# Two feed-forward layers on the unnormed x, with the reciprocal mean square put on the second product, and one plain weight tile in place of two

## The reference

```python
def rms_norm_2(x, w):
    xf = x.astype(jnp.float32)
    y = xf * lax.rsqrt(jnp.mean(xf * xf, axis=-1, keepdims=True) + RMS_EPS)
    return (y * w.astype(jnp.float32)).astype(x.dtype)

    for layer in range(DEPTH_2):
        ...
        x = x + mixed @ w_out[layer]
        h = rms_norm_2(x, mlp_norm_w[layer])
        x = x + jnp.square(jax.nn.relu(h @ w_up[layer])) @ w_down[layer]
    return rms_norm_2(x, final_norm_w)
```

## Time and profile before

| | us |
|---|---|
| median of 3 runs | 1392.38 (1392.15 to 1392.46) |
| the profiled execution, as a whole | 1391.14 |
| its span, from the first to the last instruction | 1389.4 |
| PE busy | 1369.2 (99%) |
| DVE busy | 649.9 (47%) |
| ACT busy | 263.4 (19%) |
| granted TensorE clock, mean | 0.998 |

### The profile page before, as it was taken

One profiled execution on the slowest core, in us unless ns is written; L12 is line 12 of the kernel. 1 busy time (PEld: TensorE's weight loads), 2 busy tenths in 40 slices (PEclk: granted clock), 3 DMA queues, 4 the chain that ended last, 5 costly groups with the idle time before them and its releaser, 6 DMA issues.

```text
span 1389.4 us, 21701 instructions
## 1 busy us (share of the span) xinstructions
PE 1369.2 (99%) x9138; PEld 1051.1 (76%) x9138; DVE 649.9 (47%) x1483; ACT 263.4 (19%) x561; POOL 7.2 (1%) x16
## 2 busy tenths in 40 slices
PE   9999999999999999999999999999999999999997
PEld 6888886454445444454488879999998878999997
DVE  2476554111111111111287837775446784777544
ACT  2234102000000000000143421220004352122000
POOL 0000000000000000000000000000000000000000
PEclk9999999999999999999999999999999999999999
DMA  9895667999999999999944234444544414444510
GB/s 392 352 390 227 255 242 292 421 421 420 421 421 421 420 421 420 421 421 420 421 169 152 90 118 159 179 164 171 171 163 152 152 62 150 154 168 166 177 67 32
DMA packets 51235, 362.53 MB, mean 261 GB/s; under 512 B 6064, under 2 KB 6384, under 8 KB 7872
## 3 DMA queue, kind: packets, MB, share of 16 engines
q1 hardware_dynamic: 48528, 353.39, 64.4%
q10 hardware_dynamic: 2032, 5.70, 1.4%
q0 software_dynamic: 576, 2.01, 0.4%
HBM read 357.92 MB, written 1.06 MB: 258 GB/s over the span
## 4 chain that ended last, share of the span: by engine, by line
PE 95%; DMA 3%; DVE 1%; issue 0%; SPq 0%; ACT 0%; DVEq 0%
PE bank L1096 26%; PE bank L844 23%; PE bank L546 20%; PE bank L558 5%; PE bank L854 4%; PE bank L832 4%; DMA ring<-in_weights 3%; PE bank L1241 2%; PE bank L1032 2%; PE bank L663 2%; PE bank L1145 1%; PE bank L1196 1%; PE bank L1222 1%; PE bank L1209 1%; PE bank L884 0%
## 5 line engine op out<-in xcount | busy, mean ns | idle before, releaser
L546 PE MATMUL bank<-h,ring 128*128 128x256 f32 x832 | 184.5, 381 | 0.1
L546 PEld LDWEIGHTS bank<-h,ring 128*128 128x128 f32 x832 | 156.7, 190 | 22.5 <-issue 1.5
L844 PE MATMUL bank<-ring,x_s 128*64 128x512 f32 x768 | 167.8, 592 | 1.6 <-issue 0.9
L844 PEld LDWEIGHTS bank<-ring,x_s 128*64 128x64 f32 x768 | 56.1, 137 | 110.1 <-issue 110.1
L1096 PE MATMUL bank<-hid,ring 128*128 128x128 f32 x912 | 115.6, 275 | 0.0
L1096 PE MATMUL bank<-h,ring 128*128 128x128 f32 x896 | 113.8, 275 | 0.0
L1096 PEld LDWEIGHTS bank<-hid,ring 128*128 128x128 f32 x912 | 108.6, 192 | 0.0
L1096 PEld LDWEIGHTS bank<-h,ring 128*128 128x128 f32 x896 | 107.0, 192 | 0.1
L1956 DVE TENSOR_TENSOR act<-act,bank 128x512 f32<-128x512 f32 x16 | 11.0, 687 | 195.7 <-PE bank L844 195.7
L1096 PE MATMUL bank<-sq,ring 128*128 128x128 f32 x720 | 95.1, 275 | 0.0
L1096 PEld LDWEIGHTS bank<-sq,ring 128*128 128x128 f32 x720 | 87.6, 192 | 0.0
(11 more groups left out here) (361 smaller groups left out, 1701.3 us busy)
## 6 DMA issues: line engine op xcount, KB each, us to landing
ring<-in_weights SPq DMA_DIRECT2D x288, 1024.0 KB, 12.3
ringx<-in_weights SPq DMA_DIRECT2D x48, 1024.0 KB, 19.8
x<-in_x SPq DMA_DIRECT2D x1, 1024.0 KB, 5.1
pool_a<-in_cst ACTq DMA_DIRECT2D x1, 1024.0 KB, 6.5
bias<-bias_rows POOLq DMA_DIRECT2D x1, 1024.0 KB, 16.6
ring<-cq ACTq DMA_DIRECT2D x8, 128.0 KB, 2.4
ring<-ck ACTq DMA_DIRECT2D x8, 128.0 KB, 2.4
out<-h ACTq DMA_DIRECT2D x2, 512.0 KB, 3.6
```

The costliest lines, as they stand in the source:

```text
L546: ins = e.matmul(u.ap[:, 0:S], w[:, k * width + j * P:k * width + (j + 1) * P], acts[:, k, :], start=k == 0, stop=k == kc - 1)
L844: ins = e.matmul(g.bank[bank][ex * SLOTS:(ex + 1) * SLOTS, :], stat(m)[:, ex * SLOTS:(ex + 1) * SLOTS], pair[ex][:, m * 512:(m + 1) * 512] ...
```

## The change

The feed-forward part of both layers runs on `g.xw` in place of the normed `g.h`. The reciprocal mean square `g.scr2` multiplies the result of the second product ahead of its addition to x. One tile of `w_up` is plain in place of two, and 15 run in seven products in place of 14. The square root and the scaling of `g.h` go. ACT takes over relu and square of the two plain chunks. The squares go to `g.h`. On PE the sum of the squares stands behind seven tile 1 in place of behind the first plain chunk; on the DVE the weight sums of tiles 0 and 1 stand between the additions to x, the differences are made from `g.xw`, and `dve_norm` keeps its place ahead of the loop over the seven tiles.

```diff
-UPS = 14
+PLAIN = 1
+UPS = 16 - PLAIN
 SEVENS = UPS + 15
@@ pe_layer
-    for j in range(2):
-        w = g.filled(e, layer_tile(l, 16 + j))
-        for jj in range(2):
-            oc = 2 * j + jj
-            pe_chunk(e, g, ("up", l, oc), w, jj, 256, KC, g.xw, raw(1))
-            if oc == 0:
-                pe_norm_added(e, g, n + 1)
-        g.owed += 1
+    w = g.filled(e, layer_tile(l, 16))
+    for jj in range(2):
+        pe_chunk(e, g, ("up", l, jj), w, jj, 256, KC, g.xw, raw(1))
+    g.owed += 1
     for i in range(SEVENS):
         pe_seven(e, g, l, i)
+        if i == 1:
+            pe_norm_added(e, g, n + 1)
@@ pe_seven
-    (b11, t1), (b21, b22) = token_quarters(g.h if i < UPS else g.hid[:, 8 * b:8 * b + 8, :])
+    (b11, t1), (b21, b22) = token_quarters(g.xw if i < UPS else g.hid[:, 8 * b:8 * b + 8, :])
@@ act_layer
-        e.activation(g.sq2[:, 2 * j:2 * j + 2, :], g.x[:, 2 * j:2 * j + 2, :], ACT.Square).then_inc(s["squares"], 1)
-    act_root(e, g, 3 + 2 * l, g.rs2, g.scr2)
+        e.activation(g.h[:, 2 * j:2 * j + 2, :], g.x[:, 2 * j:2 * j + 2, :], ACT.Square).then_inc(s["squares"], 1)
+    for jj in range(2):
+        ps = g.full(e, "up", l, jj)[:, 0:S]
+        g.read(("up", l, jj), e.activation(g.hid[:, jj, :], ps, ACT.Relu))
+        g.evac(e, "up", l, jj)
+    e.activation(g.hid[:, 0:2, :], g.hid[:, 0:2, :], ACT.Square).then_inc(s["hid_ready"], 1)
@@ dve_layer
-        if j > 1:
-            dve_add_squares(e, g, n + 1, j - 1, 2)
-    dve_add_squares(e, g, n + 1, 3, 2)
-    dve_weight_sums(e, g, l, 0)
+        if 1 <= j <= 2:
+            dve_weight_sums(e, g, l, j - 1)
+    e.wait_ge(s["xw"], KC * (2 * l + 2))
+    dve_differences(e, g, g.xw, g.h_diff, g.t1_last)
+    for j in range(1, 4):
+        dve_add_squares(e, g, n + 1, j, 2, g.h)
     dve_norm(e, g, n + 1, None, g.h, g.rs2, g.scr2)
-    dve_rs_scaled(e, g, n + 1)
-    e.wait_ge(s["h_scaled"], KC * (n + 2))
-    dve_differences(e, g, g.h, g.h_diff)
-    for oc in range(4):
-        ps = g.full(e, "up", l, oc)
-        g.read(("up", l, oc), e.tensor_tensor(g.hid[:, oc, :], ps[:, 0:S], g.rs2, ALU.mult))
-    for oc in range(4):
-        g.evac(e, "up", l, oc)
-        ins = e.scalar_tensor_tensor(out=g.hid[:, oc, :], in0=g.hid[:, oc, :], scalar=0.0, in1=g.hid[:, oc, :], op0=ALU.max,
-                               op1=ALU.mult)
-    step.up(ins)
-    chunks_done = step.n
-    dve_weight_sums(e, g, l, 1)
     for i in range(SEVENS):
         key, b, of = seven_block(l, i)
...
             two = g.x[:, 2 * mp:2 * mp + 2, :].rearrange("p c t -> p (c t)")
+            e.wait_ge(s["recip"], RECIPS[n + 1])
+            both = g.pair_c.rearrange("p (c t) -> p c t", c=2)
+            g.after(e)
+            step.up(e.tensor_tensor(both, both, g.scr2.unsqueeze(1).to_broadcast([P, 2, S]), ALU.mult))
+            g.after(e)
             ins = e.tensor_tensor(two, two, g.pair_c, ALU.add)
...
-        g.read(("down", l, jj), e.tensor_tensor(g.x[:, k, :], g.x[:, k, :], ps[:, 0:S], ALU.add))
+        g.read(("down", l, jj), e.tensor_tensor(g.pair_a, ps[:, 0:S], g.scr2, ALU.mult))
         g.evac(e, "down", l, jj)
+        e.tensor_tensor(g.x[:, k, :], g.x[:, k, :], g.pair_a, ALU.add).then_inc(s["x_down"], 1)
+        e.wait_ge(s["x_down"], 5 * l + 4 + jj)
```

More of the change, by code:

```diff
@@ L498 @@
 RECIPS = {0: 1, 1: 2, 2: 4, 3: 5, 4: 6, 5: 7, 6: 8}
-ROOTS = {0: 1, 1: 2, 2: 4, 3: 6, 4: 7, 5: 9, 6: 10}
+ROOTS = {0: 1, 1: 2, 2: 4, 4: 6}
 ADDED = {0: 1, 1: 2, 3: 3, 4: 4, 5: 5, 6: 6}
 def pe_norm_added(e, g, n):
-    sq = g.sq2 if n else g.sq
+    sq = {0: g.sq, 3: g.h, 5: g.h}.get(n, g.sq2)
     u = g.take(e, ("ss", n))
@@ L537, in h_ready @@
 def h_ready(e, g, n, k):
-    e.wait_ge(g.s["h_shifted" if n < 2 else "h_scaled"], KC * n + k + 1)
+    e.wait_ge(g.s["h_shifted" if n < 2 else "h_scaled"], KC * (n if n < 2 else 1 + n // 2) + k + 1)
 def pe_chunk(e, g, key, w, j, width, kc, acts, ready, bank=None):
@@ L1037, in pe_layer @@
         g.owed += 1
-    for j in range(2):
-        w = g.filled(e, layer_tile(l, 16 + j))
-        for jj in range(2):
-            oc = 2 * j + jj
-            pe_chunk(e, g, ("up", l, oc), w, jj, 256, KC, g.xw, raw(1))
-            if oc == 0:
-                pe_norm_added(e, g, n + 1)
-        g.owed += 1
+    w = g.filled(e, layer_tile(l, 16))
+    for jj in range(2):
+        pe_chunk(e, g, ("up", l, jj), w, jj, 256, KC, g.xw, raw(1))
+    g.owed += 1
     for i in range(SEVENS):
         pe_seven(e, g, l, i)
-    w = g.filled(e, layer_tile(l, 18 + SEVENS))
-    e.wait_ge(s["hid_ready"], UPS * (l + 1))
+        if i == 1:
+            pe_norm_added(e, g, n + 1)
+    w = g.filled(e, layer_tile(l, 16 + PLAIN + SEVENS))
+    e.wait_ge(s["hid_ready"], 16 * (l + 1))
     for jj in range(2):
@@ L1080, in pe_seven @@
     key, b, of = seven_block(l, i)
-    w = g.filled(e, layer_tile(l, 18 + i))
+    w = g.filled(e, layer_tile(l, 16 + PLAIN + i))
     (a11, a12), (a21, a22) = quarters(w)
     s1, s2, s3, s4 = (g.sums[i % 2][:, n * 512:(n + 1) * 512].rearrange("p (k c) -> p k c", k=4) for n in range(4))
-    (b11, t1), (b21, b22) = token_quarters(g.h if i < UPS else g.hid[:, 8 * b:8 * b + 8, :])
+    (b11, t1), (b21, b22) = token_quarters(g.xw if i < UPS else g.hid[:, 8 * b:8 * b + 8, :])
     t2, t3, t4 = g.h_diff if i < UPS else g.hid_diff[b]
-    if i >= UPS and b == 3:
+    if i < UPS or b == 3:
         t1 = g.t1_last
@@ L1499, in act_layer @@
         g.evac(e, "lout", l, j)
-        e.activation(g.sq2[:, 2 * j:2 * j + 2, :], g.x[:, 2 * j:2 * j + 2, :], ACT.Square).then_inc(s["squares"], 1)
-    act_root(e, g, 3 + 2 * l, g.rs2, g.scr2)
+        e.activation(g.h[:, 2 * j:2 * j + 2, :], g.x[:, 2 * j:2 * j + 2, :], ACT.Square).then_inc(s["squares"], 1)
[4 more added lines that the diff above has]
+    e.activation(g.hid[:, 0:2, :], g.hid[:, 0:2, :], ACT.Square).then_inc(s["hid_ready"], 1)
     for i in range(UPS):
-        two = g.hid[:, 4 + 2 * i:6 + 2 * i, :]
+        two = g.hid[:, 2 + 2 * i:4 + 2 * i, :]
         act_first_product(e, g, ("up7", l, i))
@@ L1520, in act_down @@
         act_first_product(e, g, ("down7", l, k // 2))
[L1521 to L1524, removed]
+    e.wait_ge(g.s["x_down"], 5 * l + (k // 2 if k < 6 else k - 3) + 1)
 def act_turn_halves(e, g, l, which):
@@ L2102, in dve_layer @@
     dve_layer_prob(e, g, l, 1)
-    e.wait_ge(s["root"], 5 + 3 * l)
+    e.wait_ge(s["root"], 5 + 2 * l)
     e.tensor_tensor(o, o, inv, ALU.mult).then_inc(s["o_scaled"], 1)
@@ L2145, in dve_layer @@
         if i < UPS:
-            dve_seven(e, g, key, (UPS + 4) * l + i + 1, g.hid[:, 4 + 2 * i:6 + 2 * i, :].rearrange("p c t -> p (c t)"))
+            dve_seven(e, g, key, (UPS + 4) * l + i + 1, g.hid[:, 2 + 2 * i:4 + 2 * i, :].rearrange("p c t -> p (c t)"))
         elif b == of - 1:
@@ L2158, in dve_layer @@
             ins.then_inc(s["x_down"], 1)
-            e.wait_ge(s["x_down"], 3 * l + mp + 1)
+            e.wait_ge(s["x_down"], 5 * l + mp + 1)
             for oc in (2 * mp, 2 * mp + 1):
@@ L2166, in dve_layer @@
             dve_weight_sums(e, g, l, i + 2)
-        if i in (2, 6, 10, 13):
+        if i in (3, 7, 11, 14):
             done = i // 4
-            if done == 0:
-                e.wait_ge(step.sem, chunks_done)
-            e.wait_ge(s["hid_ready"], UPS * l + 4 * done + 2)
+            e.wait_ge(s["hid_ready"], 16 * l + 4 * done + 4)
             dve_differences(e, g, g.hid[:, 8 * done:8 * done + 8, :], g.hid_diff[done], g.t1_last if done == 3 else None)
```

## The result

| | before | after |
|---|---|---|
| median, us | 1392.27 (4 runs) | 1406.49 (1405.31 to 1407.21, 4 runs) |
| span of the profiled execution, us | 1389.4 | 1405.4 |
| mean granted clock | 0.998 | 0.992 |

The ratio is 1.0106, with a 95% interval of 1.0093 to 1.0118: the change makes the kernel about 1% slower. The forecast was 1404.6 us, in a range of 1401.7 to 1407.6.

What follows compares the result with a forecast made beforehand. The prediction took PE to bound the kernel. Its terms, -1.3 (tiles) + 10.8 (pauses) + 0.46 (last chunk) + 2.2 (clock) = +12.2 us, on 1392.38 gave 1404.6 us, in a range of 1401.7 to 1407.6.

Steps and rivals of the forecast that it cites:

- What bounds the kernel: Whole span: PE is busy 99% and the last chain is PE's for 95%; DVE, ACT and weight loads are hidden.
- PE's own work: Feed-forward part: one plain tile (6.90 us) becomes a seven tile (6.253 us), -0.65 us a layer, -1.3 in all.
- The start of the seven tiles: Ahead of seven tile 0: differences ready 1.8 us early, last `xw` 0.4 us early, so no cost.
- The moved norm: Seven tile 2: PE waits for weight sums queued on the DVE behind dve_norm, 5.4 us a layer, 10.8 in all.
- The multiplication: Second product's output chunks: an extra DVE instruction, free at the third pair, +0.46 us at the end of layer 1.
- The table of the square root: Roots at layer 1's start and the end need their own 1.28 us table load, hidden, with no drain cost.
- TensorE's clock: Behind each pause the clock falls to half after 3.3 us, costing 1.1 us a layer, 2.2 in all.
- no pause at all (3): Rival at the DVE's wait ahead of the seven-tile loop: PE never pauses, 1391.5 us; chance 0.04.
- a late start (4): Rival before the seven tiles: differences or last `xw` hold PE up 0.5 to 2 us a layer, 1405.6 to 1408.6; chance 0.10.
- a clock that stays up (1): Rival: pause as forecast, but the clock stays up or falls in one layer only, 1402.3 to 1403.4 us; chance 0.27.
- A return of the clock later than half a tile (2): Rival behind the pause: over half a seven tile at low clock, 3.2 us or more a layer, 1408.5 and above; chance 0.09.

Runs made afterwards that it cites:

- late_dve: The changed kernel with dve_norm moved on the DVE from ahead of the seven-tile loop to behind the weight sums made for i = 2; 1390.45 us, ratio 0.9994 to before.
- two_plain: late_dve with two plain tiles and 14 in seven products, as the kernel before had them; 1392.99 us, ratio 1.0009 to before.
- fill: The changed kernel with 11 unread matmuls of 128x128 against 256 tokens behind the norm's product in each layer; 1402.09 us, ratio 1.0079 to before.
- early_pe: The changed kernel with the norm's product on PE behind seven tile 0 in place of tile 1; 1391.46 us, ratio 0.9999 to before.
- sums_first: The changed kernel with the weight sums of tile 2 made ahead of dve_norm on the DVE; 1396.69 us, ratio 1.0041 to before.
- fill_seven: fill with 7 unread matmuls in place of 11, leaving a pause of about 2.3 us in each layer; 1401.24 us (2 runs).

## Why the prediction was right

The time lay in the range, 1.9 us above the forecast, and the mechanism was the forecast one: two pauses of PE behind the DVE's wait, with the clock down behind each. Step by step:

- **What bounds the kernel.** PE, with every other engine hidden: right. What the change saves on the DVE and ACT brought nothing in late_dve.
- **PE's own work.** -0.65 us a layer was forecast, -0.66 is measured (late_dve and two_plain against each other and against rows 2).
- **The start of the seven tiles.** Cost at nothing: right. The last difference ended at 839.06, 2.0 us before PE began tile 0 at 841.04; forecast were 1.8. The last `xw` was written at 836.16, 0.6 us ahead of its load; forecast were 0.4.
- **The moved norm.** 5.4 us a layer were forecast, as the DVE's queue behind its wait less the first product of tile 2; 5.33 is measured in both layers. The working took five durations from rows 3 and 4, and the stretch came out at 6.21 us from the end of the product to PE's restart (854.42 to 860.63), against 6.3. What it left out is 0.27 us that PE loses at the restart beyond the wait (the 1560 instructions took 174.47 us in fill, and late_dve's 1568 took 175.09, less 0.89 for the first product). early_pe and late_dve show that either engine's order cures it, and sums_first that the queue's length sets the pause.
- **The multiplication.** In the third pair the sums were ready at 1025.02, and PE wanted them at 1025.5: no cost, with 0.5 us left of 1.2. At the end, the forecast was +0.46. From the start of the last plain tile to the end of the last product of the squares it is 8.59 us before (1372.18 to 1380.77) and 9.04 after (1388.07 to 1397.11), +0.45.
- **The table of the square root.** It moved as forecast. At layer 1's first norm the load is at 1045.40 and its root, released by the reciprocal, at 1050.18: hidden. The trace of after has, at the end:

```profile
1395.93 0.42 ACT L1598 ACTIVATE sq<-x 128x256 f32<-128x256 f32 x1 [2.93 <-DVE x L2171]
1396.36 1.28 ACT L1602 ACT_TABLE_LOAD   x1
1398.64 0.31 ACT L1602 ACTIVATE rs<-scr 128x128 f32<-128x128 f32 x1 [1.00 <-DVE scr L2340]
```

The load is new at L1602 and ends 1.00 us before the reciprocal releases the root. By an estimate with the 2.66 us of the Trainium skill ("ScalarE: Activation LUTs", "What ACT_TABLE_LOAD costs") the root could not have begun before 1396.36 + 2.66 = 1399.02; it began at 1398.64. Here the measurement decides against the drain behind the load.

- **TensorE's clock.** The mechanism was right, and the size is the term that was missed: 2.2 us in all were forecast, 2.00 + 2.56 = 4.6 are measured. The step that failed is "if the low clock lasts as long" as the fall took, 3.3 us: it lasted 6.8 us in each layer, 2.6 and 1.4 us of that still in the pause. The fall itself came 2.7 us after PE's last matmul in layer 0 and 3.9 in layer 1, on both sides of the 3.3 of rows 7. The rule of the Trainium skill ("TensorE: Matmul & The Clock Gate", "HAM oscillation") that such pauses bring the clock down held for both pauses of 5.3 us. Of the four shorter ones made in sums_first and fill_seven, one was followed by a fall.

Put together: -1.3 + 11.2 + 0.45 + 4.6 = +14.9 us by the traces (14.7 with the 0.12 between the layers and the 0.34 at the store), +14.2 by the medians, +12.2 by the forecast. Of the 2.7 us between 14.9 and 12.2 the clock has 2.4. Of the rivals, no pause at all (3), a late start (4) and a clock that stays up (1) are out. A return of the clock later than half a tile (2) is out as well, though the measured price lies between the forecast's and its own: 19 and 25 of the 56 matmul instructions of a tile ran at the low clock, a third and somewhat under a half, and the price was 2.0 and 2.6 us a layer, against 1.1 in the forecast and 3.2 for this rival.

## What to carry to other kernels

When work is moved on one engine, look at every wait for its result on the others, and at all that is queued behind that wait: here a value wanted about 113 us later was waited for ahead of sums that were wanted at once. The price of such a wait is the queue behind it less the work that the engine wanting the queue's results still has. Here it was read off a trace of the kernel before to a tenth of a us: 5.4 against 5.33, and 2.1 against 2.2 in sums_first. Behind a pause of TensorE of 5.33 us the low clock cost 2.0 and 2.6 us more, so the pause was not the whole price.

## What the runs showed of the hardware

- The granted clock fell at different times after the last matmul of a kernel: 1.3 us in late_dve (1381.72 to about 1383.0), 3.3 in before, 3.6 in after (1397.11 to about 1400.7), 4.4 in early_pe (1379.75 to about 1384.1).
- It can fall when PE is already at work again: in layer 0 of sums_first it fell 0.8 us after a pause of 2.2 us had ended.
- A stretch at the low clock under dense matmuls lasted 3.4 us (routing of after, sums_first) or, behind the pauses of 5.33 us, 6.8 us including the rest of the pause. Why one and not the other is open: no run here tells it.
- In the routing a stretch at the low clock came behind two gaps of 0.8 and 0.7 us with small matmuls between them, in some executions and not in others. With both gaps filled it was gone in all 11 executions, and with it the upper of the two groups of times, 1.6 us apart. Why one execution has it and the next not is open.
